# Output projection: the last two row-blocks by twos of outputs, with half of the sums of x1's squares among them

## The reference, cut to what matters

```
y  = group_rmsnorm(concat(y_conv, y_sgu, y_na), out_norm_g) @ w_out
x1 = x + g1 * y
h2 = rmsnorm(x1, norm2_g) * (1 + sc2) + sh2
...
x2 = x1 + g2 * peer_ffn(h2)        # product keys, 16 of 16384 experts in each of 8 heads
out = rmsnorm(x2, final_norm_g)
```

## Time and profile before

| what | us |
|---|---|
| median of 3 runs | 908.53 |
| lowest and highest of them | 907.9, 910.11 |
| the profiled execution, its own device time | 910.86 |
| its span from first to last instruction | 909.1 |
| TensorE busy in it | 870.7 (96%) |
| VectorE busy | 542.7 (60%) |
| ScalarE busy | 282.9 (31%) |

### The profile page before, as it was taken

How to read it: one execution, slowest core, us unless ns; L and a number is a source line. 1 busy time by engine, 2 the same in 40 slices (tenths; PEclk the granted TensorE clock), 3 DMA queues, 4 the chain that set the end, 5 groups by cost and what they waited for, 6 DMA issues and landing times.

```text
span 909.1 us, 18061 instructions
## 1 busy us (share of the span) xinstructions
PE 870.7 (96%) x6810; PEld 821.8 (90%) x6810; DVE 542.7 (60%) x1072; ACT 282.9 (31%) x687; POOL 259.8 (29%) x242
## 2 busy tenths in 40 slices
PE   4998998998999999999999999999999999999995
PEld 2887996696989999999999999999999999999994
DVE  4557134765369989894545888887344333334447
ACT  4453234856342111112216888880000000000002
POOL 0020001500352233337432333365232232232220
PEclk9999999999999999999999999999999999999998
DMA  9986464042462799999999999999999999999993
GB/s 370 417 321 223 149 247 161 2 186 101 154 267 87 247 382 410 410 410 381 410 410 409 408 360 323 329 330 363 410 408 409 409 409 409 409 409 408 409 410 117
DMA packets 73983, 292.73 MB, mean 322 GB/s; under 512 B 9026, under 2 KB 9154, under 8 KB 67396
## 3 DMA queue, kind: packets, MB, share of 16 engines
q1 hardware_dynamic: 36868, 159.67, 45.1%
q0 software_dynamic: 28416, 100.78, 29.3%
q10 hardware_dynamic: 8640, 31.46, 8.7%
HBM read 290.73 MB, written 1.05 MB: 321 GB/s over the span
## 4 chain that ended last, share of the span: by engine, by line
PE 49%; DMA 34%; DVE 9%; ACT 4%; issue 2%; POOL 1%; SPq 0%; DVEq 0%; ACTq 0%
DMA A<-in_peer_v,row_expert 26%; PE bank L971 26%; DMA stage<-in_peer_u_t 6%; PE bank L980 4%; PE bank L667 4%; PE bank L668 4%; PE bank L669 4%; DVE sum L1537 4%; DMA A<-in_ada_w 2%; PE bank L687 1%; DVE ring_low L1438 1%; PE bank L763 1%; DVE gate_buf L1408 1%; PE bank L704 1%; PE bank L913 1%
## 5 line engine op out<-in xcount | busy, mean ns | idle before, releaser
L971 PE MATMUL bank<-A,stage 128*128 128x160 f32 x2048 | 290.4, 300 | 3.8 <-DMA stage<-in_peer_u_t 1.8
L971 PEld LDWEIGHTS bank<-A,stage 128*128 128x128 f32 x2048 | 280.1, 190 | 8.3 <-issue 7.4
L1027 PE MATMUL bank<-A,stage 128*128 128x160 f32 x2048 | 278.3, 299 | 0.0
L1027 PEld LDWEIGHTS bank<-A,stage 128*128 128x128 f32 x2048 | 278.2, 190 | 0.0
L1537 DVE SCALAR_TENSOR_TENSOR sum<-A,row_gate,sum 128x1024 f32<-128x1024 f32 x81 | 104.1, 1285 | 133.1 <-DMA A<-in_peer_v,row_expert 127.9
L1834 POOL DMA_INDIRECT A<-in_peer_v,row_expert x84 | 82.2, 979 | 166.0 <-DVE sum L1537 149.3
L1834 POOL DMA_INDIRECT A<-in_peer_u,row_expert x80 | 86.0, 1075 | 130.5 <-DVE row_dot L1524 123.1
L1524 DVE CUSTOM_DVE_ANT_0 A<-A 128x1024 f32<-128x1024 f32 x80 | 97.8, 1222 | 42.7 <-DMA A<-in_peer_u,row_expert 32.8
L1313 ACT ACTIVATE A<-bank 128x480 f32<-128x480 f32 x1 | 0.6, 570 | 276.3 <-PE bank L1027 276.3
L1246 ACT ACTIVATE A<-bank 128x160 f32 (+1 forms) x88 | 26.7, 303 | 157.1 <-PE bank L971 142.1
L669 PE MATMUL bank<-h_hi,ring_low 128*128 128x256 f32 x240 | 68.3, 285 | 0.0
(11 more groups left out here) (259 smaller groups left out, 1226.9 us busy)
## 6 DMA issues: line engine op xcount, KB each, us to landing
stage<-in_peer_u_t SPq DMA_DIRECT2D x128, 512.0 KB
stage<-in_peer_v SPq DMA_DIRECT2D x68, 512.0 KB
stage<-in_peer_v ACTq DMA_DIRECT2D x60, 512.0 KB
A<-in_ada_w SPq DMA_DIRECT2D x14, 1024.0 KB, 7.2
A<-in_w_in SPq DMA_DIRECT2D x11, 1024.0 KB, 7.4
stage<-in_ada_w SPq DMA_DIRECT2D x10, 1024.0 KB, 7.0
A<-in_w_q SPq DMA_DIRECT2D x8, 1024.0 KB, 6.0
A<-in_w_out SPq DMA_DIRECT2D x4, 1024.0 KB, 6.0
```

Of the source, the lines that this page charges most:

```text
L971: mm = pe.matmul(o, stage[j][:, k * P:(k + 1) * P], H2[:, k, 0:ND], start=(k == 0), stop=(k == KD - 1))
L1027: mm = pe.matmul(bank[b][:, n * ND:(n + 1) * ND], stage[c % SLOTS][:, m * P:(m + 1) * P], A3[:, c, :], start=(c == 0 and n == 0), stop=(c ...
```

## The change

TensorE's instructions alone are put in another order; the same instructions are issued. The blocks k = 4 and 5 stay as they were. The blocks 6 and 7 are taken for outputs 0 and 1, then for 2 and 3, for 4 and 5, for 6 and 7. Of the sum of squares, blocks 0 and 1 stand between outputs 4, 5 and outputs 6, 7; blocks 2 and 3 stand behind outputs 6, 7, as the end of `out_projection`; blocks 4 to 7 are what is left for `second_stat`.

```diff
+            def square_sums(b):
+
+                o = opened(pe, ("stat2", 0)) if b == 0 else bank[place[("stat2", 0)][0]]
+                pe.wait_ge(x1s_ready, b + 1)
+                for m in (2 * b, 2 * b + 1):
+                    mm = pe.matmul(o[:, 0:T], ones, YS[:, m, :], start=(m == 0), stop=(m == KD - 1))
+                if b == 3:
+                    mm.then_inc(fill_sem(("stat2", 0)), 1)
+
             def out_projection():
 
-                for k in range(4, KD):
+                for k in (4, 5):
                     out_products(k, range(KD))
+                for b in range(4):
+                    for k in (6, 7):
+                        out_products(k, (2 * b, 2 * b + 1))
+                    if b >= 2:
+                        square_sums(b - 2)
 
             def second_stat():
 
-                o = opened(pe, ("stat2", 0))
-                for m in range(KD):
-                    if m % 2 == 0:
-                        pe.wait_ge(x1s_ready, m // 2 + 1)
-                    mm = pe.matmul(o[:, 0:T], ones, YS[:, m, :], start=(m == 0), stop=(m == KD - 1))
-                mm.then_inc(fill_sem(("stat2", 0)), 1)
+                square_sums(2)
+                square_sums(3)
```

## The result

The changed kernel takes 912.05 us (median of 20 runs, 909.35 to 916.19), the kernel before 910.12 in 20 runs of the same comparison. The ratio of the two is 1.0026, 95% interval 1.0014 to 1.0038: slower by 2.4 us (1.3 to 3.5), and clear of no change. The two medians by themselves are 1.9 us apart. The profiled execution has a span of 912.6 us, device time 914.40.

What follows compares the result with a forecast made beforehand. VectorE's late subtractions were taken to bound the stretch; twos and ada transfers cost nothing, the wait ahead of the squares' first pair 1.25 us, carried whole: 908.53 + 1.25 = 909.8 us, range 907.8 to 912.2.

Steps and rivals of the forecast that it cites:

- the outputs by twos: Output projection, blocks 6 and 7: banks full earlier but VectorE still busy with subtractions; gain nothing, no new wait.
- the stall: TensorE before the squares' first pair: idle 2.8 us instead of 1.34, delaying the last 12 products and sum of squares 1.25 us.
- Step (3): SyncE's two ada transfers: issued 3.9 us later, first query product 0.65 us late but hidden; no cost beside the 1.25.
- Step (4): From the sum of squares to the kernel's end: nothing absorbs the delay, so all 1.25 us carries through.
- the call of no change: Whole kernel: +1.25 us lies under about 0.3%, 2.7 us, taken as what measurement can tell; no change given 0.79.
- rival B: Gap from 205.5 to 208.32: TensorE's clock falls as well, +2.65 us, 911.2, up to +3.25, 911.8; chance 0.3.
- A: The forecast itself: the stall before the squares carries to the end, the clock holds, +1.25 us, 909.8; chance 0.45.
- three gaps that spoke for B: Elsewhere in the kernel before: TensorE stood still 3.09, 3.15 and 2.01 us and ran at half rate directly or soon after.
- The rule: Trainium skill page: gaps between matmul bursts give half rate back; by it the new gap should be avoided, time as rival B.
- dense work on both sides: Argument against rival B: around two of the long gaps TensorE did thin work, while here it is dense on both sides.

Runs made afterwards that it cites:

- relieving VectorE: The kernel before with VectorE's second subtraction of weights moved behind x1 and its third behind the scaling of h2: ratios 0.9981 and, in a second comparison, 0.9976.
- the first further profile of the changed kernel: The changed kernel unaltered, profiled once more: gap 2.79 us, clock held in this stretch, root 13.63 us after the first subtraction; whole-kernel time not used.
- the delay put in by hand: The kernel before with 48 further TensorE products between projection and squares: ratio 1.0035 (1.0021 to 1.0049), +3.2 us.
- the twos alone: The changed kernel with all four pairs of squares behind the last product, leaving only the order by twos: ratio 0.9991 (0.9975 to 1.0007).
- the gap alone: Order by twos, squares last, 10 of the last 12 products left out, against the changed kernel: gap 2.53 us, ratio 0.9996 (0.9979 to 1.0013).

## Why the prediction was right or wrong

*Right: what bounds the stretch.* VectorE, not TensorE, is late; the outputs by twos gain nothing and cost nothing (12.44 against 12.43 us), and relieving VectorE gained 2 us.

*Right: the stall.* The gap was forecast at 2.8 us and measured 2.77 to 2.79; the term was 1.25 us with bounds of 1.0 to 1.9, and it is 1.20 where the clock holds. VectorE's idle time ahead of its last pair was put at 1.2 and is 1.34.

*Right: the ada transfers are hidden.* In the first further profile of the changed kernel, without a fall, the two ada products had to wait 0.43 and 1.41 us for their data and the first query product began 220.75 - 201.50 = 19.25 us after the first subtraction (before 17.17), 0.9 us beyond the 1.20, where 0.65 was forecast; yet the first tile moved by 1.16. Step (3) holds.

*Right as far as can be told: how far it carries.* Step (4) took all of it; the delay put in by hand was carried to the end at 3.2 of 3.8 us, interval 1.9 to 4.5.

*Wrong: the call of no change.* Two steps of the prediction failed. The first is its last step: "About 0.3%, 2.7 us, is what a measurement of this kernel can tell from no change." No row was given for it. With 20 runs of each kernel the interval was 0.12% to either side, so 0.26% was told from none, and 2.4 us, which is under that line, is slower and not the same.

The second is a term of the sum. The sum took the clock's fall at nothing and left it to rival B, as if the kernel would have either A's time or B's. They are two outcomes of single executions of one program: 1.20 us to the root where the clock held, 3.85 where it fell, in two profiles each. Half and half these give 2.5 us, a quarter of falls 1.9; 2.4 was measured, and its interval of 1.3 to 3.5 leaves the share open between a few in a hundred and some nine in ten. Only the profiles and the tail of long runs, not the ratio, speak for a mixture and against A's 1.25 in every run. With the prediction's own price for B, 1.4 us beyond the stall, a quarter to a half of falls would have given 1.6 to 1.95: nearer, but still under its line of 2.7.

*Luck in the range.* The measured median, 912.05, lies inside 907.8 to 912.2. But the forecast was counted from 908.53, the median of 3 runs, and 20 runs of the kernel before put it at 910.12. From there A's time would have been 911.4, and the range 1.6 us higher.

*A size in B.* The low stretch was taken as 3.3 us, from one row of before, and the price at +2.65 in all. It lasted from about 209.4 to 216.3 and so held the whole pair, all 12 products and part of the squares behind them: +3.85, above B's upper price of 3.25. That the clock alone then cost 2.65 is a coincidence with B's figure.

*A gap that proved nothing.* One of the three gaps that spoke for B is misread. At 19.44 sixteen products took 1.94 us behind a gap of 3.09, but the same sixteen had taken as long ahead of it, from TensorE's first product of the execution on; timeline of the kernel before:

```profile
9.60 1.93 PE L687 MATMUL bank<-A,csil 128*32 128x256 f32 x16 [9.60 <-DMA A<-in_ada_w]
...
12.61 1.94 PE L687 MATMUL bank<-A,csil 128*32 128x256 f32 x16
```

So two gaps were in evidence, of 3.15 and 2.01 us, and not three.

*The rule.* The Trainium skill, page "TensorE: Matmul & The Clock Gate", section "Why this matters for your kernels", warns of gaps between bursts of matmuls, with a limit a little above the length of this one. The trace shows half rate behind a gap of 2.8 us in two of four profiles; the argument used against it, dense work on both sides, did not hold. The profiles in which the clock stayed up show that for a gap of this length it is a matter of chance, and one profile each of the kernel before and of the twos alone, with 1.34 and 1.35 us, shows no fall here.

## What to carry to other kernels

Before an engine's work is put between others to fill time, ask what is queued behind it and who waits for that: here products that would have been done in time were put behind a wait for the very engine that was already late. A gap of TensorE that grows past what the trace shows as harmless should be priced as a mixture, the fall's price by the share of executions that have it; take the share from several profiles and not from the mean clock of a run, since a fall anywhere in the kernel lowers that. Before a small forecast is called no change, ask how many runs will be compared and how wide the interval will be. Where the chain runs through another engine, its order is the one to change: two subtractions moved on VectorE gained 2 us where the change on TensorE lost 2.4.

## What the runs showed of the hardware that was not expected

A fall of the clock is not a property of the program alone but of the execution: the same gap of 2.77 to 2.79 us was followed by 0.50 of full speed in two profiles and by 1.00 in two others. When it came, the clock fell while TensorE was idle (0.72 in the window 209 to 210, with no matmul in it) and stayed at half through 6 us of uninterrupted work behind it, so the first products after a gap are not the only ones that pay. In the gap alone it was back after 3.4 us, with the squares running from 0.2 us after the fall.

A fall does not need one long gap. In the window 428 to 434 above no wait of TensorE is longer than 1.03 us, but it was busy for 2.09 of the 6 us, and at the end of that window the clock fell.
